# Two MLPs of a fused Trainium2 kernel: TensorE waits for single tiles and banks where it waited for whole stages, and the squares of four layer normalisations are partly added in pairs

## The reference, cut to what matters

```python
def _layernorm(x, g, b):
    mu = jnp.mean(x, axis=-1, keepdims=True)
    xc = x - mu
    var = jnp.mean(jnp.square(xc), axis=-1, keepdims=True)
    return xc * lax.rsqrt(var + EPS_2) * g + b

for l in range(2):
    mix = _even_mixer(h, ...) if l == 0 else _odd_mixer(h, ...)
    h = _layernorm(DN_ALPHA * h + mix, ln_mix_g[l], ln_mix_b[l])
    f = jnp.square(jax.nn.relu(h @ mlp_w1[l])) @ mlp_w2[l]     # 1024 -> 4096 -> 1024
    h = _layernorm(DN_ALPHA * h + f, ln_mlp_g[l], ln_mlp_b[l])
return h[:, N_META:]
```

## Time and profile before

| | us |
|---|---|
| median of 3 runs | 2391.2 (2390.89 to 2393.64) |
| the profiled execution, its own time | 2390.79 |
| its span in the profile | 2389.1 |
| TensorE busy | 2277.5 (95%) |
| VectorE busy | 907.0 (38%) |
| ScalarE busy | 773.2 (32%) |
| GpSimd busy | 771.4 (32%) |
| the two MLPs' matmuls, L869 and L886, in the chain that ended last | 19% and 17% of the span |

### The profile page before, as it was taken

One profiled execution on the slowest core, in us unless ns is written; L12 is line 12 of the kernel. 1 busy time (PEld: TensorE's weight loads), 2 busy tenths in 40 slices (PEclk: granted clock), 3 DMA queues, 4 the chain that ended last, 5 costly groups with the idle time before them and its releaser, 6 DMA issues.

```text
span 2389.1 us, 30500 instructions
## 1 busy us (share of the span) xinstructions
PE 2277.5 (95%) x12068; PEld 1731.3 (72%) x12068; DVE 907.0 (38%) x1362; ACT 773.2 (32%) x1154; POOL 771.4 (32%) x414
## 2 busy tenths in 40 slices
PE   7999999889999899899999999999999999999997
PEld 4776667633333479569999999888776686878875
DVE  2576553321111464424750360352000615712712
ACT  3345554211111443653421221423322425212212
POOL 3341226211111134204344444334432044444441
PEclk9899999989999999999999999999999999999999
DMA  4421114568997322102222222233222032323320
GB/s 158 142 88 54 45 45 146 229 226 355 355 376 326 129 87 80 36 10 71 80 80 90 89 86 89 80 98 96 89 76 65 9 97 71 97 88 97 97 88 36
DMA packets 69362, 278.05 MB, mean 116 GB/s; under 512 B 13017, under 2 KB 13145, under 8 KB 56961
## 3 DMA queue, kind: packets, MB, share of 16 engines
q1 hardware_dynamic: 59408, 259.61, 31.3%
q0 software_dynamic: 9552, 16.51, 2.0%
q10 hardware_dynamic: 288, 0.34, 0.1%
HBM read 323.58 MB, written 19.42 MB: 144 GB/s over the span
## 4 chain that ended last, share of the span: by engine, by line
PE 87%; issue 4%; DVE 4%; ACT 2%; POOL 2%; DMA 0%; DVEq 0%; POOLq 0%; SPq 0%; ACTq 0%
PE ps L869 19%; PE ps L886 17%; PE ps L1319 7%; PE ps L1078 5%; PE ps L522 4%; PE ps L1121 4%; PE ps L1341 4%; POOL weights_low L2686 2%; PE ps L1280 2%; PE ps L1105 2%; PE ps L533 2%; PE ps L641 2%; PE ps L1182 2%; PE ps L732 1%; PE ps L852 1%
## 5 line engine op out<-in xcount | busy, mean ns | idle before, releaser
L2686 POOL TENSOR_TENSOR weights_low<-weights,parts 128x1024 fp32r<-128x1024 f32 x250 | 630.6, 2527 | 1096.6 <-ACT parts L1869 1096.6
L869 PE MATMUL ps<-parts 128*128 128x264 f32 x2384 | 450.9, 285 | 8.1 <-DVE parts L2159 6.9
L886 PE MATMUL ps<-parts 128*128 128x512 f32 x1344 | 419.4, 392 | 9.2 <-DVE parts L2159 6.7
L1869 ACT ACTIVATE parts<-weights 128x1024 fp32r<-128x1024 f32 x257 | 269.1, 1054 | 424.4 <-PE ps L869 145.5
L869 PEld LDWEIGHTS ps<-parts 128*128 128x128 f32 x2384 | 375.6, 189 | 8.7 <-issue 8.7
L869 PE MATMUL ps<-parts,weights_low 128*128 128x264 f32 x1120 | 318.7, 285 | 0.0
L886 PEld LDWEIGHTS ps<-parts 128*128 128x128 f32 x1344 | 253.8, 189 | 65.8 <-issue 10.4
L886 PE MATMUL ps<-parts,weights_low 128*128 128x512 f32 x672 | 263.9, 393 | 0.0
L869 PEld LDWEIGHTS ps<-parts,weights_low 128*128 128x128 f32 x1120 | 212.5, 190 | 0.0
L1319 PE MATMUL ps<-area,normed 128*64 128x512 f32 x752 | 171.5, 597 | 1.6 <-DVE normed L2374 1.6
L2159 DVE TENSOR_TENSOR parts<-normed,parts 128x528 f32 (+1 forms) x64 | 152.7, 2387 | 10.1 <-DVE normed L2158 2.7
(11 more groups left out here) (458 smaller groups left out, 3612.3 us busy)
## 6 DMA issues: line engine op xcount, KB each, us to landing
weights<-in_weights SPq DMA_DIRECT2D x283, 512.0 KB, 3.5
area<-in_experts SPq DMA_DIRECT2D x141, 1024.0 KB
area<-pair_rows SPq DMA_DIRECT2D x4, 1024.0 KB, 8.0
bias_scratch<-bias_vector POOLq DMA_DIRECT2D x1, 2560.0 KB, 18.4
residual<-in_x SPq DMA_DIRECT2D x4, 512.0 KB, 6.7
area<-bias_scratch POOLq DMA_DIRECT2D x1, 2048.0 KB, 8.8
token_rows<-area SPq DMA_DIRECT2D x1, 2048.0 KB, 8.7
out_tiles<-residual SPq DMA_DIRECT2D x4, 512.0 KB, 2.8
```

Of the source, the lines that this page charges most:

```text
L869: ins = mm(ps[:, b + h, 0:HALF], wt[:, k], x[m * DT + k][:, HALF * h:HALF * h + HALF], start=m == k == j == 0, stop=m == chunks - 1 and k ...
L886: ins = mm(ps[:, b], wt[:, k], x[:, m * DT + k, first:first + SEQ], start=m == k == j == 0, stop=m == chunks - 1 and k == DT - 1 and j == 2)
L1869: fn(high_slot(n, place), RING[:, n % SLOTS], ACT.Copy).then_inc(S["w_hi"], 1)
L2686: g.tensor_tensor(RING_LOW[:, n % SLOTS], RING[:, n % SLOTS], high_slot(n, place), ALU.subtract).then_inc(S["w_lo"], 1)
```

## The change

Three things change, all inside the functions named above.

1. In `pe_mlp` the full wait stays only ahead of the first half's ups. Ahead of the second half's ups TensorE waits, for its first four outputs, for the one accumulation that frees each bank pair. Ahead of the downs there is no wait of its own: the first down output waits by `bank()` for 13 of the 16 tiles of squares, and in its second chunk once more each for the last three tiles (k = 5, 6, 7).
2. In `layer_norm` on TensorE the squares' sum reads six tiles where it read eight: 0 to 3, 4 and 6.
3. VectorE adds the squares of tile 5 to tile 4 and of tile 7 to tile 6 first, and counts a new semaphore, `sq_pair`.

```diff
-            def linear2_parts(chunks, high, low, place=IN_MLP):
+            def linear2_parts(chunks, high, low, place=IN_MLP, squares=None):
 
                 b = 2 * bank()
                 for m in range(chunks):
                     wh, wl = take_parts(place)
                     for k in range(DT):
+                        if squares and m == 1 and k >= 5:
+                            pe.wait_ge(S["dve_evac"], squares - 7 + k)
                         for h in range(2):
...
-            def linear_tokens(chunks, high, low):
-
-                linear_parts(chunks, high, low, first=0)
-
-            def linear_parts(chunks, high, low, place=IN_MLP, first=META):
+            def linear_tokens(chunks, high, low, squares=None):
+
+                linear_parts(chunks, high, low, first=0, squares=squares)
+
+            def linear_parts(chunks, high, low, place=IN_MLP, first=META, squares=None):
...
+                        if squares and m == 1 and k >= 5:
+                            pe.wait_ge(S["dve_evac"], squares - 7 + k)
...
                 ins.then_inc(S["norm_sum"], 1)
-                if len(cols) == 2:
-                    norm_sum(8, T2, 6, lambda t: X[:, t])
-                else:
-                    norm_sum(8, SEQ, 7, lambda t: X[:, t])
+                parts = [(6, 0, HALF), (7, HALF, HALF)] if len(cols) == 2 else [(7, META, SEQ)]
+                for t in (0, 1, 2, 3, 4, 6):
+                    if t < 4:
+                        pe.wait_ge(S["norm_sq"], w.next("norm_sq"))
+                    else:
+                        pe.wait_ge(S["sq_pair"], w.next("sq_pair"))
+                    for b, c, width in parts:
+                        ins = mm(ps[:, b, 0:width], ONES, X[:, t, c:c + width], start=t == 0, stop=t == 6)
+                ins.then_inc(S["norm_sum"], 1)
+                w.count("norm_sq", 4)
...
                 for half in range(2):
-                    begin_stage("act_evac")
-                    w.count("dve_evac", 16)
                     if half == 0:
+                        begin_stage("act_evac")
                         first_pair(*x, IN_MLP, cols)
                         for n in range(14):
                             linear(1, *xs)
                     else:
+                        sums = w.value("dve_evac")
+                        stage.update(n=0, evac="act_evac", nb=4)
                         with pe_loop(2, 8, act_evac=8, w_lo=8):
-                            for _ in range(8):
+                            for n in range(8):
+                                if n < 4:
+                                    pe.wait_ge(S["dve_evac"], sums - 3 + n)
                                 linear(1, *xs)
-                    begin_stage("dve_evac")
+                    w.count("dve_evac", 16)
+                    squares = w.value("dve_evac")
+                    stage.update(n=0, evac="dve_evac", nb=4)
                     with pe_loop(2, 8, dve_evac=4, w_lo=8):
-                        for _ in range(4):
-                            linear(2, *(map(tiles, f) if linear is linear2_parts else f))
+                        for n in range(4):
+                            linear(2, *(map(tiles, f) if linear is linear2_parts else f), squares=None if n else squares)
...
                     ins.then_inc(S["ln_cent"], 1)
                 w.count("norm_sum")
+                before = 8 + 1 + 8 + 8 + 8 + 3 + 8 * (2 * l + (kind == "mlp"))
+                for t in (4, 6):
+                    dve.wait_ge(S["norm_sq"], before + t + 2)
+                    v.tensor_tensor(x[:, t], x[:, t], x[:, t + 1], ALU.add).then_inc(S["sq_pair"], 1)
                 dve.wait_ge(S["norm_sd"], w.next("norm_sd"))
```

More of the change, by code:

```diff
@@ L340, in build @@
             p_in meta_in out_done ln_cent ln_out c2_in c3_in hot_in bvec_out wr_in route_x lam_exp gelu_in gelu_th
-            gelu_done xq w_hi w_lo x_hi x_lo lru_t pad_zero lru_x lru_r lru_done hidden mla_ones q_ready k_rope k_ready m_rows m_in mla_s mla_p mla_o mla_om mla_d mla_dm mla_y mla_ym ret_s ret_used ret_o ret_y decay_in sum_part hl_kept g_lo roped y_hi y_lo route_t route_c sq_added""".split()
+            gelu_done xq w_hi w_lo x_hi x_lo lru_t pad_zero lru_x lru_r lru_done hidden mla_ones q_ready k_rope k_ready m_rows m_in mla_s mla_p mla_o mla_om mla_d mla_dm mla_y mla_ym ret_s ret_used ret_o ret_y decay_in sum_part sq_pair hl_kept g_lo roped y_hi y_lo route_t route_c sq_added""".split()
         S = {n: ctx.enter_context(nc.semaphore(n)) for n in names}
```

## The result

The changed kernel took 2365.27 us in the median of its runs (2359.91 to 2366.52), the kernel before 2391.93 beside it (2390.89 to 2393.64): a ratio of 0.9884, 95% interval 0.9866 to 0.9901, so 24 to 32 us less. Forecast were 2363.2 us and a range of 2358 to 2370. The profiled execution took 2359.91 us, 30.9 less than that of before.

The account below looks back on a forecast made before the run. TensorE, busy 95% of the span, was taken to bound the kernel. 23.8 us from the MLPs plus 4.2 from the sums, 28.0 off the profiled 2390.79, gave 2362.8, as a median 2363.2 us; range 2358 to 2370.

Parts of the forecast that it names:

- TensorE bounds the stretch: 1120 to 2389 us: TensorE's pieces run end to end with only waits between, so what it gains the end gains.
- Rest and slow start are one cost: MLPs: rests plus the slow clock behind the 3.4 us ones, counted as whole stretches, 11.9 us per MLP, 23.8 in all.
- 4 x 1.6: Four MLP stretches behind 3.4 us rests: slow starts, 6.3 us; a rival, 8%, kept them for another cause than rest, 2369.5 us.
- The added waits and loop entries cost nought: MLPs: 40 added waits, each already met, and entering loops without a wait ahead were taken to cost nothing.
- The upper bound of 2.6 us for the entries: MLP loop entries: at worst 0.44 us of issue for each of six entries.
- Tile 13 to 15 come in time, the weights too: Up to down: last squares and split weights ready before TensorE wants them; rival that weights come late, slower, 2449 us, 4%.
- the 9.0 reckoned as the worst: Up to down: tile 15 done 9.0 us behind the ups if GpSimd lengthens all three operations, wanted after 10.9.
- The sums: 1.08 and 1.01 us each: Four normalisations: six tiles instead of eight gain 2 x 1.08 + 2 x 1.01 = 4.2 us; rival that pairs give nothing, 8%.
- the wait for the first pair: Squares' sums: TensorE waits 0.7 us for VectorE's first pair addition.
- GpSimd is idle there: Normalisations: GpSimd idle in all four stretches, so pair additions take about 0.7 us rather than 2.86.
- the 3 us that I gave as the dear end of a normalisation: Normalisations: with additions lengthened to 2.86 us each normalisation would lose 3 us, 12 us in all.
- The median of the runs: Whole kernel: 28.0 us off the profiled 2390.79 gives 2362.8; the median lies 0.4 above, 2363.2 us.

Follow-up runs that it names:

- before_filled5: Kernel before, with five constant float32 matmuls (3.3 us) on TensorE in each of the four rests between ups and downs, waits kept: 2384.47 us, ratio 0.9972.
- many_waits: Changed kernel plus one always-met wait ahead of each of the eight k-steps of every chunk in the MLPs and the odd layer's projections: 2362.31 us, ratio 0.9877.
- norms_only: Kernel before with only the changed squares' sums (pairs added by VectorE, six tiles on TensorE), the MLPs' waits as before: 2386.50 us, ratio 0.9976.
- gpsimd_beside2: Changed kernel with four GpSimd subtractions placed beside VectorE's two pair additions in the second normalisation: 2366.77 us, ratio 0.9898.
- the three comparisons: Three measurements of the unedited changed kernel, each beside the kernel before: 2365.27 against 2391.93, 2362.49 against 2392.19, 2363.09 against 2390.77 us.
- the two fillings that were longer than the rest: Ten constant matmuls in the up-to-down rests of the kernel before, 2395.12 us; eight behind the first three squares' sums of the changed kernel, 2364.77 us.
- before_filled: Kernel before, with ten constant float32 matmuls (6.6 us) on TensorE in each of the four rests between ups and downs, waits kept: 2395.12 us, ratio 1.0014.
- after: The changed kernel itself, first measurement and profile, against the kernel before: 2365.27 us, ratio 0.9884.

## Why the prediction was right

- **TensorE bounds the stretch, and what its waits give the end gets.** Right: the two pieces shortened by 12.0 us each, 11.9 forecast, and nothing took the place of the rests.
- **Rest and slow start are one cost.** Right, and the step that a sum over the list of waits alone would have missed: 13.6 + 2.3 = 15.9 us of waits, but 23.9 us of gain. before_filled5 shows the 6.3 us of the slow starts by themselves, forecast at 4 x 1.6. The other 1.7 us are six restarts of 0.3 us, which the forecast had in its whole stretches without naming them.
- **The added waits and loop entries cost nought.** Right: the rate in the joined pieces is that of the pieces of before, and many_waits puts over 30 times as many in for nothing. The upper bound of 2.6 us for the entries was not needed.
- **Tile 13 to 15 come in time, the weights too.** Right: no wait for L2178 (the former L2159) or for the weights in the MLPs. Tile 15 was done 4.9 us behind the ups, between the 3.0 of before and the 9.0 reckoned as the worst, 6 us before it is wanted. The mean of that line went from 2387 to 2508 ns, as GpSimd lies beside it more often; nobody waits for it.
- **The sums: 1.08 and 1.01 us each.** Right: 7.39 became 6.30 and 7.13 became 6.1, 4.3 us in all, and norms_only 4.4. A sub-step was off: the wait for the first pair was 0.4 us, not 0.7, because a record's end by the model lies behind the start of the next by 0.2 us or more, which I did not count; the end time was right, since it was reckoned from VectorE's addition.
- **GpSimd is idle there.** Right for the change; gpsimd_beside2 shows the price if it isn't. The rule of the Trainium skill (SBUF — State Buffer, Who interferes with whom) is borne out by the second addition and the first scaling, each held until GpSimd's subtraction had ended, 2.7 and 2.5 us. Of the 3 us that I gave as the dear end of a normalisation the sum lost 1.9, since only one of the two additions was caught; the scaling, which I had not counted, lost 1.8 more.
- **The median of the runs.** 28.0 us forecast; the three comparisons gave 26.7, 29.7 and 27.7. The difference to the 30.9 of the profile is the untouched part and one slow start behind a normalisation, of the size (1.7 us) that the range allowed for. The forecast's 2363.2 us lies within 2.1 us of the three medians (2365.27, 2362.49, 2363.09). As single executions of the changed kernel lie between 2359.91 and 2366.52 us, that is closer than the reasoning can claim; what it can claim is the 28.2 us between the mean and the end.

## What to carry to other kernels

When one engine bounds a stretch, price a wait of TensorE by the pieces of the chain on either side of it against an undisturbed piece's rate, not by the wait's length: here a rest of 3.4 us cost 5.2, and one of 1.2 us cost 1.4. Where a wait can't be avoided, constant matmuls into a free bank keep the clock, but size them by the records that the profile shows, since the two fillings that were longer than the rest cost more than they gained. A wait for "all of the stage" ahead of a stage that starts with its first tile should be a wait for that tile. Waits that are met were free here, between matmuls that followed one another at full speed.

## What the runs showed of the hardware

A float32 matmul of 384 columns has two records, one every 0.32 us, so it takes 0.65 us (before_filled: 20 records in 6.6 us). After rests of the same 3.1 us behind the sums, the first 32 matmuls of the third normalisation's L905 took 7.5, 9.1 or 10.4 us in different profiles, so the slow start of TensorE (1.2 GHz in place of 2.4) costs nought, 1.6 or 2.9 us there (granted clock over those matmuls 1.00 in after, 0.70 in gpsimd_beside2), while behind the 3.4 us rests of the MLPs all eight that before and norms_only show cost 1.4 to 1.6 us against the pieces behind the short wait. A rest of 1.2 us brought no slow start. 1352 met waits on TensorE, 169 of them records of 0.051 us, left the MLPs' pieces as they were to 0.01 us.
